# A reordered start, ropes between weight units on GpSimd, and three early down products in a hybrid decoder layer on one Trainium2 core

## The chip, the core and the metric

The kernel runs on one core of a Trainium2 chip (trn2). TensorE multiplies; VectorE (DVE in the profile), ScalarE (ACT) and GpSimd (POOL) do the rest; SyncE (SP) issues most of the DMAs. Each engine works through its own queue in order and waits on counting semaphores. The metric is the device time of one execution in microseconds (us).

## The reference

A decoder layer over 528 tokens (16 learned meta tokens and 512 of the sequence) of width 1024, in float32:

```python
h = concat([meta, x])                                   # (528, 1024)
h = h + 0.5 * swiglu(rmsnorm(h, ffn1_norm), gate, up, down)      # FFN1, D_FF = 2816
h = h + token_mixing(rmsnorm(h, mix_norm), ...)                  # mixer
h = h + 0.5 * swiglu(rmsnorm(h, ffn2_norm), gate, up, down)      # FFN2
return rmsnorm(h, final_norm)[16:]

def swiglu(h, w_gate, w_up, w_down):
    return (silu(h @ w_gate) * (h @ w_up)) @ w_down
```

`token_mixing` projects with `w_in` and runs two mixers side by side: a gated linear attention of 4 heads (`gq`, `gk`, `gv`, `gr`), and a sparse attention of 8 heads (`dq`, `dk`, `dv`), whose keys an indexer selects (the best 128 of each query's visible keys). `dq` and `dk` get rotary embeddings, `x * cos + rot(x) * sin`, with `rot` swapping the halves of each head of 64. Both results, side by side, are multiplied with `w_out`.

## The kernel before

**Splitting.** Every large product is made of three passes on values rounded to the type fp32r: the high part of the weights with the high part of the input, high with low, and low with high. ScalarE makes a high part of a weight unit (128 columns for all 1024 rows) with `hi(u)`, GpSimd the low part with `lo(u)` (line 1796), in pieces of 256 columns: four operations for a full unit, two for a down unit. `w_hi` and `w_split` count them. TensorE counts `w_used` when it is through with a unit, and this frees its place. `raw` is a ring of four slots that SP refills in the order of the units, each slot when its unit is split.

**The start.** `x` is loaded with tokens on partitions. TensorE turns it in ten steps (line 2724); VectorE copies each result out of PSUM with `keep_x(n)` (line 461) into `h`; ScalarE squares and sums; VectorE makes variance and reciprocal in two parts (`x_variance(0)` for the meta tokens and the first two tiles, `x_variance(1)` for the last two), ScalarE the root; the reciprocal roots stand on diagonals (`diag`), which TensorE multiplies with ones (`spread`, line 2712) to have them across all partitions. VectorE makes eight tiles `xn` (line 2394) from `h`, gain and spread. ScalarE makes `xh` (`high_x(d)`, line 1932) and VectorE `xl` (line 2399).

**The first four products** (`first_products`, line 2498) are gate and up of the first two plain tiles of FFN1, units 0 to 3. Each has 16 matmuls of 264 columns for each of its three passes. TensorE begins with the high passes of units 0 and 1 tile by tile, as ScalarE delivers `xh`, with unit 0's low pass two tiles behind; then the low pass of unit 1, the high passes of 2 and 3, the low passes of 2 and 3, and at last the `xl` passes of all four.

**FFNs.** The first group of four column tiles (`PLAIN = 4`) is computed plainly, the others in pairs with seven products of half size instead of eight (`SEVEN`, line 2673), with sums of weight quarters made by VectorE (`sums`, `low_pair`). The gate product is passed through Silu on ScalarE, multiplied with the up product on VectorE, and split again into `ah` (line 1946) and `al` (line 2204). The down products of the first group follow its last plain tile: four of the eight (`PRE_DOWN = 4`), each a sum over the four activation tiles. The activation of the last plain tile is the latest, so the loop over `(k0, k1, ds)` runs tiles 0 to 2 of down products 0 and 1 first, then their tile 3 (which waits for `a_lo`), and then down products 2 and 3 in full. Down product d of this group has PSUM bank 2d; banks 4 to 7 hold the last plain tile's gate and up, so that products 2 and 3 wait until that tile is out (`a_prod` in FFN1, `up_scaled` in FFN2). VectorE adds each finished down product to `h` (`add_down`, line 2229).

**The mixer.** Units in order: indexer queries (4), indexer keys, `gv` (4), `dq` and `dk` (8, `M_DQK`), `dv` (4, `M_DV`), `gq` and `gk` (4, `M_GQK`), `gr` (4), `w_out` (8). The first two DQK products and a part of the third and fourth run between the indexer's logits; then DQK 4 to 7 (48 matmuls of 264 columns each, line 2462), the four V units (30 of 512 columns, line 582), and the attention. ScalarE takes DQK product n out of PSUM into `pjb[:, n]` (`pj_kept`), SP swaps its halves by DMA into `sw[:, n % 4]` (`swap_r`: after the product's eviction, and for n of 4 and more after rope n - 4 is complete, since it reuses the buffer), and GpSimd applies the rope n in three operations: `sw * sin`, `pjb * cos`, their sum (`q_roped`). In GpSimd's queue rope n stands whole behind the low part of unit DQK 3 + n. Meanwhile VectorE selects the top keys, from 456 to 522 us, without a wait on TensorE.

**The attention.** TensorE waits for all eight ropes (`q_roped` 8), makes the first two heads' logits (line 722), and fills the rest of its time with products that the linear attention needs (`fill_step`: `M_GQK` and the first two `gr` units, one product of 8 steps for every 4 pairs of heads). The fill products have the banks of `FILL_BANK`; the first has bank 0, where V's first block was, and so waits for `v_kept` 4. The tails (`tails`, line 734), the last 16 keys' logits of the first block of queries, run after fill steps 1 and 2. `turn_probs(n, t)` turns a head's probabilities into bank 4 or 5. VectorE masks (`masked`, lines 1404 and 1409), evicts fill products (`keep_fill`), and shares the eviction of turned probabilities with ScalarE.

## Time and profile before

| | |
|---|---|
| median of 3 runs | 1056.43 us (1056.31 to 1061.72) |
| the profiled execution | 1057.6 us |
| its span, first to last instruction | 1055.8 us |
| TensorE busy | 1037.3 us, 98% |
| granted TensorE clock | 0.999 |
| GpSimd, VectorE, ScalarE busy | 659.6, 783.1, 466.8 us |
| DMA engines, mean share of the span | 32.8% |

The profiled execution is one run with the profiler on; its span leaves out 1.8 us around the instructions. PE is TensorE's matmuls, PEld its weight loads, which overlap. A matmul's end is modelled, and successive matmuls overlap, so that the distance of two starts is what one costs. In a timeline a row is a run of like instructions: start, time to the end of the last, engine, line, operation, out<-in, shapes, count, and in brackets the idle time of the engine before it and what ended that.

### The profile page before, as it was taken

The numbers are of one execution on the slowest core, as the hardware profiler recorded it, in microseconds if no ns is written. First come the engines' busy times: TensorE is split into PE (matmuls) and PEld (weight loads), VectorE is DVE, ScalarE is ACT, GpSimd is POOL, SyncE is SP. The second block draws the span as 40 slices with busy tenths as digits, with TensorE's granted clock in tenths as the row PEclk, the third lists the DMA queues.
The fourth block names the chain that finished last, engine by engine and source line by source line (L and its number), as shares of the span: only waits on it lengthen the run. The fifth ranks groups of instructions, "written<-read, shape, count | busy, mean of one in ns | idle before, by whom it ended". The sixth has DMA issues, their size and how long they took to land.

```text
span 1055.8 us, 19800 instructions
## 1 busy us (share of the span) xinstructions
PE 1037.3 (98%) x7527; PEld 947.1 (90%) x7527; DVE 783.1 (74%) x1270; ACT 466.8 (44%) x748; POOL 659.6 (62%) x747
## 2 busy tenths in 40 slices
PE   8999999999999999989999999999999999999997
PEld 8999999999999997878678788778899999999997
DVE  7557897677676587699766585478999977777835
ACT  6433444334343344562256536353544433443436
POOL 5767777787786367259732213446887877777840
PEclk9999999999999999999999999999999999999999
DMA  6243343333332444334321102222233434334322
GB/s 202 71 119 102 84 112 96 111 87 105 110 95 77 119 120 111 83 100 122 100 61 41 41 21 61 62 78 77 84 100 101 120 111 117 86 106 112 91 61 80
DMA packets 172258, 98.71 MB, mean 93 GB/s; under 512 B 6787, under 2 KB 167606, under 8 KB 172166
## 3 DMA queue, kind: packets, MB, share of 16 engines
q1 hardware_dynamic: 172064, 97.38, 32.8%
q8 instruction: 60, 0.98, 0.4%
q14 instruction: 32, 0.26, 0.1%
q10 hardware_dynamic: 102, 0.08, 0.0%
HBM read 91.18 MB, written 2.10 MB: 88 GB/s over the span
## 4 chain that ended last, share of the span: by engine, by line
PE 89%; POOL 4%; DVE 2%; ACT 2%; issue 2%; DMA 0%; SPq 0%; DVEq 0%; ACTq 0%; POOLq 0%
PE ps L2462 37%; PE ps L2673 34%; PE ps L582 5%; PE ps L596 4%; POOL wl L1796 2%; PE ps L766 1%; PE ps L722 1%; PE ps L2498 1%; PE ps L745 1%; PE ps L878 1%; POOL pjb L1879 1%; POOL sw L1876 1%; POOL pjb L1877 1%; PE ps L2724 1%; DVE xn L2394 1%
## 5 line engine op out<-in xcount | busy, mean ns | idle before, releaser
L1796 POOL TENSOR_TENSOR wl<-raw,wh 128x256 fp32r<-128x256 f32 x292 | 249.4, 888 | 203.2 <-ACT wh L1905 167.3
L1796 POOL TENSOR_TENSOR wxl<-raw,wxh 128x256 fp32r<-128x256 f32 x240 | 231.2, 988 | 136.6 <-ACT wxh L1905 136.1
L2462 PE MATMUL ps<-ah,wxh 128*128 128x264 f32 (+2 forms) x464 | 123.2, 319 | 0.4 <-DVE al L2204 0.4
L2462 PE MATMUL ps<-ah,wxl 128*128 128x264 f32 (+2 forms) x464 | 123.0, 318 | 0.0
L2462 PE MATMUL ps<-al,wxh 128*128 128x264 f32 (+2 forms) x464 | 122.9, 318 | 0.0
L2673 PE MATMUL ps<-xh,wh 128*128 128x264 f32 (+1 forms) x360 | 101.9, 283 | 0.0
L2673 PE MATMUL ps<-xl,wh 128*128 128x264 f32 (+1 forms) x360 | 101.9, 283 | 0.0
L2673 PE MATMUL ps<-xh,wl 128*128 128x264 f32 (+1 forms) x360 | 101.5, 282 | 0.0
L2229 DVE SCALAR_TENSOR_TENSOR h<-ps,h 128x528 f32<-128x528 f32 (+1 forms) x88 | 61.0, 694 | 51.9 <-PE ps L2462 51.8
L2462 PE MATMUL ps<-xh,wh 128*128 128x264 f32 (+3 forms) x304 | 94.5, 349 | 4.7 <-POOL wl L1796 3.5
L2462 PE MATMUL ps<-xl,wh 128*128 128x264 f32 (+3 forms) x304 | 90.8, 337 | 0.0
L2462 PE MATMUL ps<-xh,wl 128*128 128x264 f32 (+3 forms) x304 | 90.7, 337 | 0.0
L1905 ACT ACTIVATE wxh<-raw 128x512 fp32r<-128x512 f32 (+2 forms) x88 | 53.4, 607 | 73.5 <-PE ps L2462 72.8
L2462 PEld LDWEIGHTS ps<-ah,wxl 128*128 128x128 f32 x464 | 77.1, 188 | 6.3
L2462 PEld LDWEIGHTS ps<-ah,wxh 128*128 128x128 f32 x464 | 77.1, 188 | 5.7 <-DVE al L2204 0.9
L2462 PEld LDWEIGHTS ps<-al,wxh 128*128 128x128 f32 x464 | 77.2, 188 | 4.8
L1796 POOL TENSOR_TENSOR wl<-ws,wh 128x256 fp32r<-128x256 f32 x72 | 69.9, 1001 | 9.5 <-ACT wh L1923 9.5
L1946 ACT ACTIVATE ah<-ubuf 128x528 fp32r<-128x528 f32 (+1 forms) x36 | 23.0, 640 | 110.7 <-DVE ubuf L2337 100.1
L1905 ACT ACTIVATE wh<-raw 128x1024 fp32r<-128x1024 f32 (+1 forms) x61 | 57.9, 968 | 23.5 <-PE ps L582 18.1
L2673 PEld LDWEIGHTS ps<-xh,wh 128*128 128x128 f32 x360 | 67.8, 188 | 0.4
L2673 PEld LDWEIGHTS ps<-xl,wh 128*128 128x128 f32 x360 | 67.8, 188 | 0.4
L2673 PEld LDWEIGHTS ps<-xh,wl 128*128 128x128 f32 x360 | 67.9, 189 | 0.0
(322 smaller groups left out, 3016.7 us busy)
## 6 DMA issues: line engine op xcount, KB each, us to landing
raw<-in_ffn_w_gate SPq DMA_DIRECT2D x44, 512.0 KB, 4.1
raw<-in_ffn_w_up SPq DMA_DIRECT2D x44, 512.0 KB, 4.9
raw<-in_ffn_w_down SPq DMA_DIRECT2D x80, 256.0 KB, 2.8
raw<-in_w_in SPq DMA_DIRECT2D x28, 512.0 KB, 4.2
raw<-in_w_out SPq DMA_DIRECT2D x8, 512.0 KB, 3.4
xin<-in_x SPq DMA_DIRECT2D x4, 512.0 KB, 5.7
raw<-in_ffn_w_down SPq DMA_DIRECT2D x16, 128.0 KB, 2.2
out<-xin SPq DMA_DIRECT2D x4, 512.0 KB, 3.5
```

Of the source, the lines that this page charges most:

```text
L582: mm = pe.matmul(ps[0:n, V_BANKS[m0][b], :], xx[:, 2 * q + k, s:s + n], ww[:, slot, k * 512:(k + 1) * 512], start=(q == 0 and k == 0 and c ...
L596: return pe.matmul(ps[:, bank, :], ww[:, slot, k * 256 + dd * P:k * 256 + (dd + 1) * P], rr[:, tile, META:TOK], start=(starts and k == 0 a ...
L722: pe.matmul(ps[0:w, qk_bank(n), 0:main_keys(b)], pjb[e:e + HD, pair, s:s + w], pjb[e:e + HD, 4 + pair, 0:main_keys(b)], start=True, stop=T ...
L745: mm = pe.transpose(ps[0:wc, 4 + t % 2, c * w:(c + 1) * w], lg[0:w, n % 4, sc:sc + wc], ident[0:w, 0:w])
L766: mm = pe.matmul(o[HD * e:HD * (e + 1), :], dv[0:wc, c, (hd + e) * HD:(hd + e + 1) * HD], pt[0:wc, (n + e) % 3, c * w:(c + 1) * w], start= ...
L878: mm = pe.matmul(ps[:, lv_bank(g) + e, c:c + 64], x, x.rearrange("p (m a b) -> p m a b", a=2, b=LEVELS[g - 1])[:, :, 1, :], start=True, st ...
L1796: op = pool.tensor_tensor(dst[:, part], src[:, part], high[:, part].bitcast(F32), ALU.subtract)
L1905: act.activation(places(0, PLACE[u], c)[:, 0:n], raw[:, slot, 0:n], ACT.Copy).then_inc(w_hi, c)
L1946: act.activation(ah[:, j, tk], src, ACT.Copy).then_inc(a_hi, 1)
L2229: dve.scalar_tensor_tensor(out=as_parts(h[:, d, tk], norm), in0=psum_parts(bank, norm), scalar=0.5, in1=as_parts(h[:, d, tk], norm), op0=A ...
L2462: mm = pe.matmul(ps[0:m, bank + a, 0:width], places(lo, PLACE[u], -(-WIDTH[u] // HALF_UNIT))[:, k * P:k * P + m], r[:, tile, t:t + width], ...
L2673: mm = pe.matmul(ps[:, seven_bank(v, i), 0:w], places(lo, at_p[wn], 1)[:, k * P:(k + 1) * P], x_operand(xlo, xn_, w, number)[:, k, :], sta ...
```

## The change

It has three parts.

1. The start. VectorE's `keep_x(8)` goes to ScalarE, behind the last two diagonals and ahead of `hi(0)`; `x_variance(1)` comes after `keep_x(6)` instead of after `keep_x(7)`; `high_x(0)` stands between `hi(0)` and `hi(1)`. In TensorE's loop unit 1's high pass is one tile behind unit 0's. The `xl` passes of units 0 and 1 come ahead of the low pass of unit 2, and that of unit 2 ahead of the low pass of unit 3.
2. The mixer. GpSimd's low part of DQK 4 comes ahead of rope 0; after it, two of the ropes' 24 operations stand between two low parts, three from V 1 on, and the last two behind the low part of `M_GQK` + 1. The first fill product has bank 5 and no wait for `v_kept` 4 (the second, in bank 1, has it now); the second head's turned probabilities, in bank 5, wait for its eviction; the tails run after fill steps 2 and 3.
3. Both FFNs. Tiles 0 to 2 of three down products instead of two run ahead of tile 3.

```diff
@@ keep_x
+            if n == X_BY_ACT:                                   # X_BY_ACT = 8
+                eng.activation(dst, src, ACT.Copy).then_inc(x_kept_act, 1)
+            else:
+                eng.tensor_copy(dst, src).then_inc(x_kept, 1)
@@ ScalarE, start
+            keep_x(act, X_BY_ACT)
             hi(0)
+            high_x(0)
             hi(1)
-            for d in range(KT):
+            for d in range(1, KT):
                 high_x(d)
@@ VectorE, start
             for n in range(10):
-                keep_x(dve, n)
+                if n != X_BY_ACT:
+                    keep_x(dve, n)
...
-                if n == 7:
+                if n == 6:
                     x_variance(1)
...
-            dve.wait_ge(x_kept, 10)
+            dve.wait_ge(x_kept, 9)
+            dve.wait_ge(x_kept_act, 1)
@@ first_products
                 for k in range(KT + 2):
                     if k < KT:
                         part(0, k, 0)
-                        part(1, k, 0)
+                    if k >= 1 and k <= KT:
+                        part(1, k - 1, 0)
                     if k >= 2:
                         part(0, k - 2, 1)
-                for v, lo in ((1, 1), (2, 0), (3, 0), (2, 1), (3, 1)):
+                for v, lo in ((1, 1), (2, 0), (3, 0)):
                     for k in range(KT):
                         part(v, k, lo)
-                for v in range(4):
+                low_inputs(0)
+                low_inputs(1)
+                for v in (2, 3):
                     for k in range(KT):
-                        mm = part(v, k, 0, True)
-                    mm.then_inc(w_used, 2)
+                        part(v, k, 1)
+                    low_inputs(v)
@@ GpSimd, mixer
-            for n in range(8):
-                lo(U_MIX + M_DQK + 3 + n)
-                pool.wait_ge(swapped[5 + n], 64)
...
-            lo(U_MIX + M_DV + 3)
-            lo(U_MIX + M_GQK)
+            def rope_steps(first, last):                        # operation i is step i % 3 of rope i // 3
...
+            lo(U_MIX + M_DQK + 3)
+            lo(U_MIX + M_DQK + 4)
+            for n in range(4):
+                rope_steps(2 * n, 2 * n + 2)
+                lo(U_MIX + M_DQK + 5 + n)
+            rope_steps(8, 10)
+            for n in range(4):
+                lo(U_MIX + M_DQK + 9 + n)
+                rope_steps(10 + 3 * n, 13 + 3 * n)
             lo(U_MIX + M_GQK + 1)
+            rope_steps(22, 24)
             lo(U_MIX + M_GQK + 2)
@@ attention
-            FILL_BANK = [0, 1, 0, 0, 0, 1]
+            FILL_BANK = [5, 1, 0, 0, 0, 1]
...
-                    if m == 0:
+                    if m == 1:
                         pe.wait_ge(v_kept, 4)
...
                 if t >= 2:
                     turn_free(pe, t - 2)
+                elif t == 1:
+                    pe.wait_ge(gqk_scaled, 1)
...
-                if k in (1, 2):
-                    tails(k - 1)
+                if k in (2, 3):
+                    tails(k - 2)
@@ FFN, down products of the first group
-                for k0, k1, ds in ((0, PLAIN - 1, range(2)), (PLAIN - 1, PLAIN, range(2)), (0, PLAIN, range(2, PRE_DOWN))):
+                for k0, k1, ds in ((0, PLAIN - 1, range(3)), (PLAIN - 1, PLAIN, range(3)), (0, PLAIN, range(3, PRE_DOWN))):
```

In all parts the same values are computed; only their order and the engine of one copy differ.

## Rows read from the trace of the kernel before

**Rows 1.** the page, busy time of each engine (share of the span, instructions)
```profile
PE 1037.3 (98%) x7527; PEld 947.1 (90%) x7527; DVE 783.1 (74%) x1270; ACT 466.8 (44%) x748; POOL 659.6 (62%) x747
```

**Rows 2.** TensorE's waits: line waited for; us in total, times, longest
```profile
PE ps L2462 <- POOL wl L1796: 3.5, 3, 2.3
PE ps L2498 <- POOL wl L1796: 2.0, 1, 2.0
...
PE ps L2462 <- ACT pjb L1055: 0.7, 1, 0.7
PE ps L582 <- POOL wl L1796: 0.6, 1, 0.6
```

**Rows 3.** TensorE in three stretches: us, busy (matmuls), granted clock, DMA
```profile
31.53:41.33 9.80, 9.80 (x80) 1.00 0.19 55
...
495.71:523.54 27.83, 27.83 (x120) 1.00 0.42 110
475.57:481.39 5.82, 5.82 (x47) 1.00 0.51 138
```

**Rows 4.** GpSimd's timeline from 20 us: start, duration, what, [idle before it]
```profile
20.97 10.51 POOL L1796 TENSOR_TENSOR wl<-raw,wh 128x256 fp32r<-128x256 f32 x8 [0.48 <-ACT wh L1905]
```

**Rows 5.** VectorE's timeline of the start
```profile
19.18 8.31 DVE L2399 TENSOR_TENSOR xl<-xn,xh 128x528 fp32r<-128x528 f32 x8
...
9.97 1.89 DVE L461 COPY h<-ps 128x512 f32<-128x512 f32 x3
...
13.77 1.44 DVE L2394 SCALAR_TENSOR_TENSOR xn<-h,vecs,ps 128x528 f32<-128x528 f32 x2 [0.35 <-PE ps L2712]
```

**Rows 6.** ScalarE's timeline of the start, to 15.9 us
```profile
12.41 0.69 ACT L2084 ACTIVATE diag<-ident,xvar 128x128 f32<-128x128 f32 x2
13.01 1.99 ACT L1905 ACTIVATE wh<-raw 128x1024 fp32r<-128x1024 f32 x2
14.90 1.16 ACT L1932 ACTIVATE xh<-xn 128x528 fp32r<-128x528 f32 x2
```

**Rows 7.** ScalarE's timeline around the mixer's first DQK copies
```profile
457.47 0.62 ACT L1051 ACTIVATE pjb<-ps 128x512 f32<-128x512 f32 x1
457.95 1.09 ACT L1905 ACTIVATE wh<-raw 128x1024 fp32r<-128x1024 f32 x1
```

**Rows 8.** TensorE's timeline of the start
```profile
6.26 3.67 PE L2724 MATMUL ps<-ident,xin 128*128 128x128 f32 x16
...
9.72 2.00 PE L2724 MATMUL ps<-ident,xin 128*128 128x128 f32 x16
...
15.67 1.74 PE L2498 MATMUL ps<-xh,wh 128*128 128x264 f32 x12 [1.14 <-ACT xh L1932]
```

**Rows 9.** GpSimd's timeline of the ropes and low parts
```profile
462.06 1.30 POOL L1876 TENSOR_TENSOR sw<-sw,cs 128x512 f32<-128x512 f32 x1 [11.30 <-DMA sw<-pjb]
...
465.96 2.79 POOL L1796 TENSOR_TENSOR wl<-raw,wh 128x256 fp32r<-128x256 f32 x4
...
488.85 1.34 POOL L1876 TENSOR_TENSOR sw<-sw,cs 128x528 f32<-128x528 f32 x1
...
513.18 8.43 POOL L1796 TENSOR_TENSOR wl<-raw,wh 128x256 fp32r<-128x256 f32 x12
```

**Rows 10.** TensorE's timeline, the first matmul of the first fill product
```profile
525.06 0.47 PE L2462 MATMUL ps<-xh,wh 128*128 128x512 f32 x1 [0.41 <-ACT dv L1063]
```

**Rows 11.** VectorE's timeline, the first operation after the top-k work
```profile
529.38 0.18 DVE L1404 CUSTOM_DVE_ANT_0 lg<-ps,mask 100x16 f32<-100x16 f32 x1 [7.18 <-PE ps L734]
```

**Rows 12.** TensorE's timeline, FFN2's last plain tile
```profile
747.33 0.50 PE L2462 MATMUL ps<-ah,wxh 128*128 128x512 f32 x1 [0.43 <-DVE al L2204]
```

**Rows 13.** VectorE's timeline at FFN2's and at FFN1's last plain tile
```profile
743.51 0.68 DVE L2266 TENSOR_TENSOR t<-ps,rstd 128x512 f32<-128x512 f32 x1
...
70.11 0.71 DVE L2229 SCALAR_TENSOR_TENSOR h<-ps,h 128x528 f32<-128x528 f32 x1 [0.35 <-PE ps L2462]
```

**Rows 14.** GpSimd's timeline behind FFN2's last plain tile
```profile
750.39 4.70 POOL L1796 TENSOR_TENSOR wl<-ws,wh 128x256 fp32r<-128x256 f32 x4 [3.66 <-ACT wh L1923]
```

More of the change, by code:

```diff
@@ L454, in build @@
         X_BANKS, VEC_BANK = 6, 4
+        X_BY_ACT = 8
         def keep_x(eng, n):
@@ L1442, in keep_fill @@
                 else:
-                    bank = [0, 1, 0, 0, 0, 1, 6, 7][m]
+                    bank = [5, 1, 0, 0, 0, 1, 6, 7][m]
                     dst = pja[:, 4 + m, :] if m < 4 else gr[(m - 4) // 2][:, m % 2, :]
@@ L1869, in _ @@
                 lo(U_MIX + M_DQK + n)
-            for n in range(8):
-                lo(U_MIX + M_DQK + 3 + n)
-                pool.wait_ge(swapped[5 + n], 64)
-                c = META if n < 4 else 0
-                s, r = sw[:, n % 4, c:], pjb[:, n, c:]
-                pool.tensor_tensor(s, s, sinr[:, c:], ALU.mult).then_inc(q_part, 1)
-                pool.tensor_tensor(r, r, cosr[:, c:], ALU.mult).then_inc(q_part, 1)
-                pool.wait_ge(q_part, 2 * (n + 1))
-                pool.tensor_tensor(r, r, s, ALU.add).then_inc(q_roped, 1)
-            lo(U_MIX + M_DV + 3)
-            lo(U_MIX + M_GQK)
+            def rope_steps(first, last):
+                for i in range(first, last):
+                    n, step = divmod(i, 3)
+                    c = META if n < 4 else 0
+                    s, r = sw[:, n % 4, c:], pjb[:, n, c:]
+                    if step == 0:
+                        pool.wait_ge(swapped[5 + n], 64)
+                        pool.tensor_tensor(s, s, sinr[:, c:], ALU.mult).then_inc(q_part, 1)
+                    elif step == 1:
+                        pool.tensor_tensor(r, r, cosr[:, c:], ALU.mult).then_inc(q_part, 1)
+                    else:
+                        pool.wait_ge(q_part, 2 * (n + 1))
+                        pool.tensor_tensor(r, r, s, ALU.add).then_inc(q_roped, 1)
+            lo(U_MIX + M_DQK + 3)
[7 more added lines that the diff above has]
+                rope_steps(10 + 3 * n, 13 + 3 * n)
             lo(U_MIX + M_GQK + 1)
+            rope_steps(22, 24)
             lo(U_MIX + M_GQK + 2)
@@ L2501, in part, with low_inputs @@
                     return mm
+                def low_inputs(v):
+                    for k in range(KT):
+                        mm = part(v, k, 0, True)
+                    mm.then_inc(w_used, 2)
                 for k in range(KT + 2):
```

3 lines of the change are left out of this document (1 added, 2 removed).

## The prediction

> **What bounds the kernel now.** I read first the page's busy shares. TensorE's matmuls fill 98% of the span [rows 1], so the time is the sum of TensorE's work and of its stalls, and an edit pays only where it removes a stall of TensorE or adds one. Nothing in the diff removes a matmul. The second view was therefore the waits of TensorE alone. They are few and short, and most of them lie where the diff is [rows 2]: one of 2.0 us among the first four products, on GpSimd's low part of a weight unit; three (3.5 us together), one of 0.6 us and one of 0.7 us around the DQK and V units of the mixer; and two of 0.4 us, on `dv` and on `al`, of which below. These 7.6 us are what can be won.
>
> An idle time in these rows runs from the modelled end of the last matmul, not from the moment at which the next could have started. A 264-column matmul lasts 0.28 us in the rows and starts every 0.1225 us (9.80 us for 80), a 512-column one starts every 0.232 us (27.83 us for 120) [rows 3]. So each gap loses some 0.16 us more than its idle time, and the first matmul after it is slow by some hundredths: I add 0.2 us per gap.
>
> Third came the timelines of the engines that end those waits.
>
> **The start.** GpSimd makes the low parts of units 2 and 3 in eight operations of 1.31 us, to 31.48 [rows 4]; TensorE gets the last at 31.53 [rows 3] and could have had it 2.2 us earlier. After the change the products of `xl` with units 0 and 1 (32 matmuls, 3.9 us at the rate of [rows 3]) stand ahead of unit 2's low part and 16 more ahead of unit 3's. With the 48 matmuls of the interleaved loop done at 21.9 (below) and 1.96 us for each 16, unit 2's low part is wanted at 31.7 and unit 3's at 35.7, 4 us after it is there. The `xl` tiles are now wanted from 27.8 on instead of from 33.6; VectorE has made the last of the eight by 27.49 [rows 5]. The stall goes: 2.0 + 0.2 = 2.2 us.
>
> Against that stands ScalarE's new order. VectorE's copies out of PSUM take 1.89/3 = 0.63 us each, and the variance comes one copy earlier, so the root and the two diagonals of ScalarE end at 12.5 instead of 13.1 [rows 6]. Then ScalarE has `keep_x(8)`: the trace has no such copy there; the nearest one is 0.62 us long [rows 7], and neighbours overlap by 0.09 us. I take 0.53; ends 0.5 and 1.0 (that of a conversion twice as large). So `hi(0)` starts at 12.95, as before (13.01). It takes 0.95, and `high_x(0)` follows at once at 14.0 (VectorE's first `xn` needs 0.76 and starts at some 13.2, when both the spread and the ScalarE copy are there): TensorE starts at 14.75, 0.9 us earlier than at 15.67 [rows 8]. But it gets two matmuls only. `hi(1)` stands between `high_x(0)` and `high_x(1)`, and the second tile is there at 16.1 instead of 16.06, TensorE goes on at 16.24. From there 46 of the 48 matmuls of the interleaved loop remain, 5.65 us, to 21.9; before, 48 from 15.67 came to 21.6. The later `xh` tiles come every 0.54 (1.16 less 0.62) to 0.68 us (VectorE's pace, 1.44 less 0.76) and a step of three products takes 0.73, so they hold nothing up. The early start is worth nothing and the interleaving costs 0.3 us. Net gain at the start 1.9 us (1.2 to 2.3).
>
> Does it last? Behind the first products the weight conversions, ScalarE's Silu and the loads all hang on counts that TensorE or GpSimd gives, and in FFN1 TensorE has no listed wait. The shift is handed on.
>
> **GpSimd's ropes.** Before, GpSimd has made the low part of DQK 3 by 450.8 and then sits 11.3 us until the swapped rows of rope 0 land at 462.06 [rows 9]. The high part of DQK 4 is there at 459.04 [rows 7], but its low part is queued behind rope 0, runs at 465.96 to 468.75, and TensorE stalls 2.3 us for it. Then each turn of one rope (3.9 us) and one low part (2.8 us) is 6.7 us against TensorE's 5.9 us for a product of 48 matmuls (5.82 us for 47 [rows 3]), so it stalls 0.6 us four times more. That the row of 0.7 us names `pjb` hides this: it stands in the same beat of 6.7 us.
>
> After: low part of DQK 4 at 459.1 to 461.9, in the idle time. Then two thirds of a rope (2.6 us) between low parts: 5.4 us a turn, under 5.9. Low parts of DQK 5, 6, 7 are done at 467.5, 472.8, 478.2 and wanted at 472.4, 478.3, 484.1 (TensorE can start DQK 4 at 468.9 less the stall, 466.5, and takes 5.9 each); that of V 0 is done at 483.6 and wanted at 490.0; V 1 to 3 with three operations between (6.8 us a turn) at 489, 496, 503, wanted at 497, 504, 511. All five stalls go: 4.7 + 5 x 0.2 = 5.7 us.
>
> What is late next is the last rope, since three low parts more now stand ahead of its end. From 462.06 GpSimd has four ropes of 3.9 us, four of 528 columns at 4.0 (3 x 1.34) and nine low parts of 2.8 (8.43 us for three): 15.6 + 16.0 + 25.2 = 56.8 us, to 518.9. TensorE is through V at 523.54 - 5.7 = 517.8 and waits for `q_roped` 8 before the first logits: a new wait of some 1.1 us. Gain at the first logits 4.6 us (3.6 to 5.7). The swaps on SP are not in the way: swap n waits for its product's eviction and for rope n - 4, and the last is issued at about 492 for a rope that begins at about 511. Loads now queue behind earlier low parts, thus earlier.
>
> `FILL_BANK[0] = 5` lets the first fill product start without `v_kept` 4: the 0.41 us before 525.06 [rows 10] go. The tails, one step later, wait for `v_kept` 6 at 520.4 (four copies of 0.6 us after V) and start at 522.3: nothing. VectorE's first masked logits come at about 525.1 instead of 529.38; its top-k work was done 7.2 us before those [rows 11], at 522.2, so it isn't the bound, with 2.9 us to spare. The new wait of the second head's transposes for `gqk_scaled` 1 is on an eviction that VectorE makes right after the fill product, 1.8 us ahead. Sum of this part 5.0 us (3.8 to 6.1).
>
> **Three down products.** In FFN2 TensorE runs two products of three tiles, then waits 0.43 us for the low part of the last activation (747.33 [rows 12]). A third one (9 matmuls, 2.1 us) covers this. It needs the last up product scaled, 743.51 + 0.68 = 744.2 [rows 13], and is reached at 746.7. Gain 0.6 us. Behind it GpSimd's low part for the second of the seven products lands at 755.09 [rows 14] and would be wanted at 755.15: up to 0.1 us comes back. In FFN1 there is no stall to cover: the first finished down product comes 2.2 us later, VectorE's add of 70.11 [rows 13] waits for it, and its `low_pair` slides to 75.5, still ahead of 79.4 where TensorE wants it. Worth 0. This part: 0.6 us (0 to 0.7).
>
> **Sum.** 1.9 + 5.0 + 0.6 = 7.5 us off the profiled execution's 1057.6, which gives 1050.1. That execution lies 1.2 us above the median of the runs, 1056.43: forecast 1049.0 us. At the good ends the gain is 9.4 us (1047.0), at the bad ends 5.0 (1051.4).
>
> **Rivals.**
> (a) A new wait of TensorE takes back 2 to 5 us: GpSimd ends its ropes later than 518.9, or a low part is late in the attention. For it: the margin there is already negative by 1.1 us. Against: all its prices are start to start in the same stretch. 1051 to 1054, some 1052.5.
> (b) VectorE sets the pace of the attention, so that what TensorE wins ahead of it is lost there. For it: the masks and half of the transposed probabilities are its work. Against: its idle time of 7.2 us [rows 11], and that TensorE has one wait of over 0.15 us on it in the first half of the attention. Only 1.9 + 0.6 stay: 1053.9.
> (c) The clock. TensorE runs the same transposes every 0.22 us (3.67 for 16) up to 9.7 and every 0.115 us (2.00 for 16) from there on [rows 8], the low and the full level of 1.2 and 2.4 GHz. After the change TensorE does little between 13.9 and 16.2: its two new matmuls stand alone in a gap of 2.3 us, where it was idle for 1.14 us before. If the clock fell there for as long as it was low at first (8.3 us from its first matmul), half of that is lost: 4.2 us, 1053.2. The Trainium skill, "TensorE: Matmul & The Clock Gate", section "HAM oscillation — how this bites in real kernels", says that idle stretches between bursts can put the array back to the lower clock. The trace shows none after the stall of 2.3 us at 466.6: the granted clock is 1.00 in the stretches behind it [rows 3]. That speaks against (c).
> (d) Slower than before: GpSimd is slowed in the ropes' stretch as it is at 20.97, where an operation takes 1.31 instead of 0.70 us beside VectorE [rows 4]. Its 56.8 us would have to grow by 7.5 us, 13%, to eat the whole gain; if the 36 operations of the nine low parts took 1.31, it is 22 us, and the time 1071. Against: the order alone is new, and the top-k work ran beside GpSimd's 0.70 us through the whole stretch. The Trainium skill, "SBUF — State Buffer", section "Who interferes with whom", says that a VectorE operation with two SBUF inputs and a GpSimd operation that reads SBUF block one another. The trace agrees at the start, where 1.31 us stand beside `xl` with its two inputs. The ropes' end at 518.9 lies inside the top-k work, before its end at 522.2.
>
> **From these to the numbers.** Forecast with its own ends 0.70 (range 1047.0 to 1051.1), (a) 0.12, (b) 0.09, (c) 0.04, (d) 0.05. A measurement tells 0.5% (5.3 us) from no change, so the border is at 1051.1. Faster: 0.70 and less than half of (a), 0.75. Same: the rest of (a), (b) and (c), 0.20. Slower: 0.05. The range takes in (a): 1046.8 to 1053.0; (b), (d) and part of (c), under 0.2, stay out.
>
> **What would show it.** Start: no idle time of TensorE on `wl` at 29 to 32; two matmuls at 14.7 and the next at 16.2; the first matmul of the third gate product at 39.4 instead of 41.3. Mixer: no wait on GpSimd between the DQK units; one new wait of about 1 us in front of the first logits, on GpSimd's `pjb`; fill product begins without a gap. FFN2: no wait on `al`. Wrong would be: an idle time in front of the logits of over 3 us, a new wait on the low parts of V units, a lower granted clock between 14 and 20 us, or new waits of TensorE on VectorE in the attention.

## The result, and the profile after

The changed kernel took 1050.12 us in the median of 6 runs (1049.34 to 1057.75), the one before 1057.02 (1056.26 to 1061.72); the ratio is 0.9944, with an interval of 0.9926 to 0.9961. The forecast was 1049.0 us, with a range of 1046.8 to 1053.0. Built once more for the experiments, the same kernel had a ratio of 0.9963 (0.9949 to 0.9977), and its executions lay between 1049.31 and 1056.76. So the gain is real, it is 4 to 6 us, and single executions differ by more than that. Where this spread comes from turned out to be the larger part of the study. A ratio here is not the quotient of the two medians beside it (1050.12 / 1057.02 would be 0.9935), so nothing should be read from a difference of 0.001 between the two. Two executions, one of `ropes_alone` with 1119 us at a mean granted clock of 0.85 and one of `after_s1_early` with 1259 us at 0.75, are left out of the ratios.

The profiled execution took 1050.75 us, with a span of 1049.0, against 1057.6 and 1055.8 before. First the page's busy times and then TensorE's waits, which answer to [rows 1, 2]:

```profile
PE 1036.0 (99%) x7527; PEld 946.5 (90%) x7527; DVE 779.9 (74%) x1269; ACT 467.0 (45%) x749; POOL 657.4 (63%) x747
```

```profile
PE ps L2525 <- ACT xh L1955: 1.8, 2, 0.9
...
PE ps L727 <- POOL pjb L1892: 1.0, 1, 1.0
...
PE ps L2489 <- POOL wxl L1804: 0.3, 1, 0.3
```

All waits on the low parts `wl`, 6.1 us in five places before, are gone, and with them the 0.7 us put down to `pjb` in the same beat. New are a second wait on `xh` at the start, one of 1.0 us on the last rope, and one of 0.3 us on a down unit's low part, `wxl`.

The same stretches of TensorE's work before and after give the balance. Each boundary is the start of the same matmul in both traces. The windows of after, for TensorE alone (from:to, length, busy with the number of matmuls, granted clock, DMA share, GB/s):

```profile
15.29:39.90 24.61, 24.61 (x191) 0.93 0.34 98
...
39.90:465.04 425.14, 424.74 (x3218) 1.00 0.36 100
465.04:517.24 52.20, 51.17 (x314) 1.00 0.50 134
...
517.24:526.05 8.81, 8.81 (x44) 1.00 0.25 70
...
526.05:735.81 209.76, 207.79 (x1512) 1.00 0.18 55
735.81:746.91 11.10, 11.10 (x49) 1.00 0.10 28
746.91:760.40 13.49, 13.18 (x97) 1.00 0.42 117
760.40:1041.69 281.29, 281.29 (x2023) 1.00 0.34 96
```

| stretch | before, us | after, us | gain |
|---|---|---|---|
| start to the end of the first four products | 41.33 | 39.90 | 1.43 |
| to DQK 4 | 425.14 | 425.14 | 0 |
| DQK 4 to 7 and V, to the first logits | 57.07 | 52.20 | 4.87 |
| first logits and first fill product | 9.28 | 8.81 | 0.47 |
| attention, FFN2's plain tiles | 209.76 | 209.76 | 0 |
| FFN2's early down products and the tile behind | 11.82 | 11.10 | 0.72 |
| the next seven products of FFN2 | 12.76 | 13.49 | -0.73 |
| FFN2's rest | 281.29 | 281.29 | 0 |

The sum is 6.76 us. Three long stretches, 916 us, came out the same to 0.01 us: TensorE hands a shift on unchanged, and whatever differs does so in the few places that the diff touches. The last part's gain is given back in the very next stretch. And in the first row of the windows the granted clock is 0.93.

**The start.** TensorE's timeline (start, duration, line, operation, count, idle time before and what ended it), and a window for it alone, from the fall of the clock to its rise:

```profile
13.90 0.48 PE L2525 MATMUL ps<-xh,wh 128*128 128x264 f32 x2 [0.85 <-ACT xh L1955]
15.29 1.02 PE L2525 MATMUL ps<-xh,wh 128*128 128x264 f32 x3 [0.91 <-ACT xh L1955]
```

```profile
15.33:18.75 3.42, 3.42 (x16) 0.50 0.48 132
```

Two matmuls stand alone between two idle times, as forecast. Then TensorE's clock is at its low level of 1.2 GHz for 3.4 us, right behind the second idle time; from 18.75 on it is 2.4 GHz again. The stretch from the third matmul to the end takes 24.61 us. An execution without this fall (`after_repeat`, below) takes 23.13: the fall costs 1.5 us.

**The mixer.** GpSimd's low part of DQK 4, and at the end that of the second GQK unit and the last two rope steps; then TensorE's first logits:

```profile
457.69 2.84 POOL L1804 TENSOR_TENSOR wl<-raw,wh 128x256 fp32r<-128x256 f32 x4 [8.35 <-ACT wh L1928]
...
511.67 2.83 POOL L1804 TENSOR_TENSOR wl<-raw,wh 128x256 fp32r<-128x256 f32 x4
514.47 1.34 POOL L1889 TENSOR_TENSOR pjb<-pjb,cs 128x528 f32<-128x528 f32 x1
515.88 1.30 POOL L1892 TENSOR_TENSOR pjb<-pjb,sw 128x528 f32<-128x528 f32 x1
```

```profile
517.24 1.11 PE L727 MATMUL ps<-pjb 64*100 64x512 f32 x4 [1.03 <-POOL pjb L1892]
```

The low part of DQK 4 now fills GpSimd's idle time, and the last rope ends at 517.2. TensorE, done with V, waits 1.03 us for it. VectorE's first masked logits, for [rows 11]:

```profile
523.32 0.17 DVE L1412 CUSTOM_DVE_ANT_0 lg<-ps,mask 100x16 f32<-100x16 f32 x1 [3.98 <-PE ps L739]
```

VectorE is still early, but with 4.0 us to spare where it had 7.2.

**FFN2.** TensorE and GpSimd behind the last plain tile, for [rows 12, 14]:

```profile
751.80 0.51 PE L2489 MATMUL ps<-ah,wxh 128*128 128x512 f32 x1 [0.31 <-POOL wxl L1804]
```

```profile
743.64 4.69 POOL L1804 TENSOR_TENSOR wl<-ws,wh 128x256 fp32r<-128x256 f32 x4 [3.66 <-ACT wh L1946]
748.29 8.63 POOL L1804 TENSOR_TENSOR wxl<-raw,wxh 128x256 fp32r<-128x256 f32 x6
```

The wait on `al` is gone. 4.9 us after the early products, TensorE waits for the low part of the fifth down unit: its two pieces are the first two of the six `wxl` operations and end at 751.75. Before the change they ended at 758.50 and TensorE wanted them at 758.66.

### The profile page after: what moved, and what is told of

It is laid out like the page before. It is cut to its first block, busy times and chain, and to the rows that moved or that the text cites. A ratio compares the mean times of both kernels' runs of the same rounds, so it can differ in the third digit from the quotient of the medians.

```text
span 1049.0 us, 19801 instructions
## 1 busy us (share of the span) xinstructions
PE 1036.0 (99%) x7527; PEld 946.5 (90%) x7527; DVE 779.9 (74%) x1269; ACT 467.0 (45%) x749; POOL 657.4 (63%) x747
## 4 chain that ended last, share of the span: by engine, by line
PE 86%; POOL 6%; ACT 2%; DVE 2%; issue 2%; DMA 1%; SPq 0%; DVEq 0%; ACTq 0%; POOLq 0%
PE ps L2489 36%; PE ps L2709 34%; PE ps L601 4%; POOL wl L1804 3%; PE ps L587 3%; PE ps L2525 2%; PE ps L774 1%; PE ps L727 1%; POOL pjb L1892 1%; POOL sw L1887 1%; POOL pjb L1889 1%; PE ps L753 1%; PE ps L886 1%; DMA xin<-in_x 1%; PE ps L927 0%
## 5 line engine op out<-in xcount | busy, mean ns | idle before, releaser
L1804 POOL TENSOR_TENSOR wl<-ws,wh 128x256 fp32r<-128x256 f32 x72 | 67.3, 967 | 9.5 <-ACT wh L1946 9.5
```

The lines of the kernel that those rows point to most:

```text
L1804: op = pool.tensor_tensor(dst[:, part], src[:, part], high[:, part].bitcast(F32), ALU.subtract)
```

## Experiments

Twelve kernels were run in four groups; each group had its own runs of the kernel before on the same chip, and the ratios are against those.

### The three parts, each alone

`mixer_alone` is the kernel before with part 2 of the change, `start_alone` with part 1, `down_alone` with part 3. The last one's edit:

```diff
-for k0, k1, ds in ((0, PLAIN - 1, range(2)), (PLAIN - 1, PLAIN, range(2)), (0, PLAIN, range(2, PRE_DOWN))):
+for k0, k1, ds in ((0, PLAIN - 1, range(3)), (PLAIN - 1, PLAIN, range(3)), (0, PLAIN, range(3, PRE_DOWN))):
```

> The kernel before with the second part of the change alone (GpSimd's ropes between low parts, bank 5 for the first fill product, tails a step later). My theory, from the profile after the change: this part carries 5.3 us of the whole, so 1057.0 becomes 1051.7 (ratio 0.995). The trace should show the new wait of 1.0 us on the last rope before the first logits. Rival, that VectorE's pace in the attention or something behind it takes part of it back: under 4 us.

> The kernel before with the first part alone (start). My theory: removing the stall on unit 3's low part gives 2.2 us, the interleaving takes 0.3 us, and where the granted clock falls to the lower level behind the two lone matmuls another 1.5 us are lost in that execution. So 1.9 us faster in executions with a clock of 0.999 and 0.4 us in those with 0.997. Rival: the fall of the clock is chance and has nothing to do with the new idle times; then it is seen as often in runs of the kernel before.

> The kernel before with the third part alone (three down products ahead of the last activation's tile). My theory, from the profile after the change: the stall of 0.43 us on the activation's low part goes, and TensorE waits the same time longer for the low part of the fifth down unit, so 0.0 us. As predicted before the result was known: 0.6 us faster. In the trace the idle time on wxl behind the third of the seven products tells them apart, 0.3 us or none.

| kernel | median, us | before, us | ratio | interval |
|---|---|---|---|---|
| `mixer_alone` | 1052.35 | 1056.45 | 0.9958 | 0.9939 to 0.9977 |
| `start_alone` | 1057.8 | 1056.45 | 0.9999 | 0.9988 to 1.0011 |
| `down_alone` | 1057.57 | 1056.45 | 1.0000 | 0.9991 to 1.0009 |

The mixer's part carries the gain: 4.4 us (0.0042 of 1056), under the 5.3 of the theory and over the rival's bound of 4. Its profile has the new wait, 1.3 us on `pjb`.

The down products are worth nothing. (The medians lie 1.1 us apart because the executions of both kernels fall into two groups, at 1056.1 to 1056.6 and at 1057.5 to 1058.1, and the median stands in one or the other; of this below.) Their wait is moved, as TensorE's waits and timeline in `down_alone` show: no row on `al` any more, and

```profile
757.50 0.50 PE L2462 MATMUL ps<-ah,wxh 128*128 128x512 f32 x1 [0.31 <-POOL wxl L1796]
```

The start's part has a ratio of 0.9999 too, although in its profile the first four products end at 39.64 instead of 41.33. That profile has a fall of the clock, but elsewhere, directly behind the stall of 2.25 us on DQK 4's low part, which this kernel still has at 467 us:

```profile
466.96:470.37 3.41, 3.17 (x14) 0.50 0.64 181
```

Of its 12 executions two took 1054.5 us at a mean granted clock of 0.998, three 1055.8 to 1056.1 at 0.997, and seven 1057.8 to 1058.4 at 0.996 to 0.997. One fall of 3.4 us lowers the mean by 0.0016, so the means fit one fall more in the seven than in the two. They don't prove it: in every profile the clock is also at its low level for the last 1.1 to 4.2 us, when TensorE has no matmul left; this costs nothing, but lowers the mean by 0.0005 to 0.0020. Of the 3.3 us between the fastest executions and the seven, some 1.1 can be a late first rise of the clock (last section) and 1.5 a fall at the start; the rest is open, and none of the seven has a trace. So the question became what brings the falls, and `start_old_interleave` was made for it.

### The interleaving at the start

`after_old_interleave` is the changed kernel with units 0 and 1 in step again:

```diff
             hi(0)
-            high_x(0)
             hi(1)
-            for d in range(1, KT):
+            for d in range(KT):
                 high_x(d)
...
                     if k < KT:
                         part(0, k, 0)
-                    if k >= 1 and k <= KT:
-                        part(1, k - 1, 0)
+                        part(1, k, 0)
```

> The changed kernel with two details of its start undone: high_x(0) stands behind hi(1) again, and unit 1's high pass runs beside unit 0's again. All else, the copy on ScalarE and the new order of the xl passes too, stays. My theory: TensorE starts once, without a gap in the middle, the 0.3 us come back, and the granted clock does not fall at 15 to 19 us; 1050.1 becomes 1049.1 in the median, and 0.3 us against executions of the changed kernel with a clock of 0.999. Rival: the early start is worth its place, and this is 0.5 us slower.

The kernel took 1049.41 us in the median, ratio 0.9925 (0.9910 to 0.9941), the best of all kernels, though its interval overlaps that of the changed kernel's first runs (0.9926 to 0.9961) and leaves only that of `after_repeat` (from 0.9949) apart; four of its six executions lay between 1049.37 and 1049.43. TensorE's idle time is one of 1.6 us instead of two, no fall follows it, and the first four products end at 38.15. The profile is of the one execution of 1053.55 us; its 4.2 us above the others are about a wait of 2.77 us for VectorE (last section) and a fall of the clock right behind that wait, at 528.11. `start_old_interleave` puts the same two edits on `start_alone`:

> The start's part alone on the kernel before, without its interleaving: the copy of the ninth turned tile on ScalarE and the new order of the four products behind the first loop, but units 0 and 1 in step and ScalarE's second weight unit ahead of the first activation tile, as before. The start's part with its interleaving had a ratio of 0.9999, though in its profile the first four products end 1.9 us earlier; the mean granted clock of most of its executions was 0.996 where the kernel before has 0.998 to 0.999. My theory: the stall of 2.2 us for the low part is gone in both, and the interleaving's gaps are what lowers the clock in most executions (1.5 to 1.7 us for each fall of 3.4 us). Then this kernel runs at 0.998 to 0.999, and is 1.9 to 2.3 us shorter than the one before: 1054.2 to 1055.7 us, ratio 0.998. Rival: an earlier arrival at the stall of 2.25 us at 467 us, or another place in the mixer, meets the falls, whatever the first loop is; then the ratio is again 0.999 to 1.000 and the clock 0.996 to 0.997.

It took 1054.9 us (1054.11 to 1055.38) beside 1057.66 for the kernel before, ratio 0.9975 (0.9965 to 0.9984), where `start_alone` had 0.9999. The intervals don't touch. TensorE's timeline and the window of the first four products:

```profile
14.69 1.49 PE L2506 MATMUL ps<-xh,wh 128*128 128x264 f32 x10 [1.61 <-ACT xh L1937]
```

```profile
14.69:38.07 23.38, 23.38 (x192) 1.00 0.39 110
```

Without the interleaving the start's part is worth 2.6 us (0.0025 of 1057), and the interleaving takes that away again. That the fastest executions of the two kernels lie only 0.4 us apart (1054.11 and 1054.49) says how: the interleaving costs 0.4 us where nothing else happens, and the rest lies in how often the executions of some microseconds more come. My theory's direction held; that falls of the clock are what makes these longer is argued from the profiles with a fall, as said. One of its numbers didn't hold: the mean clock is 0.997 to 0.998, not 0.998 to 0.999, and this profile too has one fall, at 452.8 us. Behind it the kernel waits for GpSimd's low parts anyway: the stall of 2.3 us is 0.7 here. A fall ahead of a stall is hidden in it.

`after_warm` fills both idle times with matmuls that nothing reads (nine `keep_warm` instead of four behind the spread, eight between the first two product matmuls and the third):

```diff
+                    if k == 1:
+                        keep_warm(8)
...
-            keep_warm(4)
+            keep_warm(9)
```

> The changed kernel with nine instead of four filler matmuls behind the spread and eight more between the first two product matmuls and the third, so that TensorE is not idle between 13.9 and 15.3 us; the fillers write a bank that nothing reads. If the fall of the granted clock at 15.3 us in the changed kernel's profile comes from the idle time in front of it, the first four products end at the full rate, 38.2 to 38.6 us where the changed kernel's profile has 39.9, and the kernel is up to 1.5 us shorter than the changed one in those executions in which the fall is there. Rival: the fall comes with or without the gap (as it did at 453 and at 528 us elsewhere); then the fillers cost 0 to 0.4 us and the median is that of the changed kernel.

Its timeline:

```profile
13.91 0.49 PE L2525 MATMUL ps<-xh,wh 128*128 128x264 f32 x2
14.24 1.95 PE L2737 MATMUL ps<-ident,ones 128*128 128x128 f32 x16
15.94 0.73 PE L2525 MATMUL ps<-xh,wh 128*128 128x264 f32 x4
```

There is no fall at the start, and the products end at 39.02, against 39.90. But the fillers run to 15.94 where the second tile is there at 15.29, so 0.65 of the 1.5 us are spent on them. The five executions agree to 0.4 us (1049.94 to 1050.33; ratio 0.9935, 0.9922 to 0.9947), and the median is that of the changed kernel. `warm_rope_first` has fillers cut to the gaps (eight behind the spread, four between the products), and the ropes' end first, of which next:

> The changed kernel with the new interleaving, the last rope steps first, and fillers cut to the gaps at the start (eight behind the spread, four between the first two product matmuls and the third; 112 ns for each of their two passes), so that they end at 15.1 us, ahead of the second tile at 15.3. If the fillers keep the clock and cost nothing, the first four products end 0.2 to 0.6 us earlier than with the longer fillers (39.0 in that profile) and the kernel takes 1048.3 to 1048.7 us. Rival: any work of TensorE in the gap delays the tile by its own queue and the interleaving still costs 0.3 us against the old one: 1048.7 to 1049.2.

Ratio 0.9938 (0.9925 to 0.9951), median 1049.82, above both what was expected and its rival, and with 1048.22 the shortest execution of all kernels. Its profile has no fall before the last microseconds. The first four products take 23.17 us from the third matmul, at 16.56, to 39.73; `after_repeat`, whose clock rose as late, has 16.53 and 39.66. So short fillers cost nothing that shows. The spread from 1048.2 to 1051.8 at the same mean clock is more than the 1.1 us of a late rise, and stays unexplained.

`after_repeat` is the changed kernel once more.

> The changed kernel once more, on the chip of the other two, to compare with. If the fall of the granted clock behind the gap at the start is a property of the new interleaving, this profile shows it again within 1 us of the third product matmul and the first four products take 24.6 us from there as they did (23.1 us without it). Rival: the fall was an accident of one execution; then none is seen before 20 us and the products end at 38.4 to 38.6 us when the clock rises early.

Median 1052.26, ratio 0.9963 (0.9949 to 0.9977). Here the rival was right for the profile: the two gaps are there, and no fall behind them.

```profile
16.53:39.66 23.13, 23.13 (x191) 1.00 0.36 103
```

So in these traces the gaps make the fall possible and not certain. Of the five profiles with the two gaps three have it (`after` at 15.33, `after_rope_first` at 17.95, `after_s1_early` at 16.69, each within 0.8 us of the third matmul), two don't; of the two with fillers and the seven with one gap none has it. What else decides is open.

`after_repeat` has a fall at 453.41. Five other profiles have one between 452.8 and 457.0 (`after_warm`, `old_rope_first`, `after_old_interleave`, `start_old_interleave`, `after_s1_early`), the other eight have none there. TensorE's timeline:

```profile
451.58 2.14 PE L688 MATMUL ps<-ikga,wa 16*128 16x264 f32 x8 [0.32 <-ACT gb L1098]
453.65 0.79 PE L2489 MATMUL ps<-xh,wh 128*128 128x512 f32 x1
454.25 0.63 PE L2489 MATMUL ps<-xl,wh 128*128 128x512 f32 x1
```

An idle time of 0.3 us and eight matmuls over 16 rows stand there, in every profile; behind them the 512-column matmuls take 0.42 us from start to start, instead of the 0.23 of the rows behind 457. Here too the same code is followed by a fall in one execution and not in another.

### The wait before the logits

`ropes_alone` is the kernel before with GpSimd's order only, without the fill product's bank and the later tails.

> The kernel before with only GpSimd's order of ropes and low parts changed. The mixer's part alone gave a ratio of 0.9958; of its 4.9 us at the logits all should be the order's and 0.4 to 0.5 us behind them the fill product's bank. So this one gains 4.5 to 4.9 us at the first logits, keeps the idle time of 0.4 us ahead of the fill product (TensorE on VectorE's last V copy), and its median is 0.4 us above that of the mixer's part alone. Rival: the bank and the later tails are needed for the gain, because without them TensorE waits for VectorE's V copies longer than before: then the wait ahead of the fill product grows to over 1 us and the gain is below 4 us.

Ratio 0.9961 (0.9948 to 0.9974), where `mixer_alone` had 0.9958. Its timeline at the logits:

```profile
517.55 1.10 PE L722 MATMUL ps<-pjb 64*100 64x512 f32 x4 [1.04 <-POOL pjb L1884]
518.59 0.50 PE L2477 MATMUL ps<-xh,wh 128*128 128x512 f32 x1
```

The new wait is the same, and the fill product follows 1.04 us after the logits' start without an idle time, bank 0 or not. In `mixer_alone` these are 519.12 and 520.16, again 1.04. Both the expectation and its rival were wrong: the 0.41 us of [rows 10] went because TensorE stood 1 us for the rope, in which VectorE's copies of V were done. The bank and the tails are worth nothing in this order.

`after_rope_first` has the last two rope steps ahead of the second GQK unit's low part:

```diff
-            lo(U_MIX + M_GQK + 1)
             rope_steps(22, 24)
+            lo(U_MIX + M_GQK + 1)
```

> The changed kernel with GpSimd's last two rope steps ahead of the low part of the second GQK unit. My theory of the new wait: the 1.0 us that TensorE waits for the last rope before the first logits is there only because three low parts more stand ahead of that rope's end. Then the rope ends some 2.8 us earlier (at about 514.4 where it was 517.2), TensorE finds it done, and the kernel is 1.0 to 1.2 us shorter than the changed one: 1048.2 to 1049.1 us, ratio to the kernel before about 0.992 to 0.993, with no wait on GpSimd in front of the logits. Rival, VectorE sets the pace there: VectorE's first masked logits wait for its own top-k work, so the wait only changes its name (TensorE on VectorE at the second pair's transposes) and the time stays at that of the changed kernel, 1049.3 to 1050.1.

The wait is gone, and nothing takes its place. GpSimd, TensorE, and the window from the matmul behind `gb` to the first product with `dv` (busy times of PE, PEld, DVE, ACT, POOL, then TensorE's clock):

```profile
515.06 1.33 POOL L1892 TENSOR_TENSOR pjb<-pjb,sw 128x528 f32<-128x528 f32 x1
516.35 2.82 POOL L1804 TENSOR_TENSOR wl<-raw,wh 128x256 fp32r<-128x256 f32 x4
```

```profile
518.19 1.10 PE L727 MATMUL ps<-pjb 64*100 64x512 f32 x4
```

```profile
453.88:531.88 78.00, 77.74 (x436) 62.70 (x437) 73.24 (x226) 32.82 (x46) 64.45 (x72) 1.00 0.45 122
```

The changed kernel takes 79.09 us for the same stretch (451.83 to 530.92): 1.09 us saved, as forecast, and the rival of VectorE falls. Yet the median is 1049.95, ratio 0.9936 (0.9923 to 0.9949), outside the 1048.2 to 1049.1 expected and not better than the changed kernel by anything that can be told. The profiled execution, of 1051.75 us, has the fall at 17.95, which has nothing to do with the ropes. `old_rope_first`, which adds the old interleaving, shows what else there is.

> The changed kernel with the old interleaving of the first two products and GpSimd's last two rope steps ahead of the low part of the second GQK unit. My theory: the stall before the logits is worth 1.1 us and the old interleaving keeps the clock up behind the start, so most executions take 1048.2 to 1048.5 us, 1.1 below the changed kernel's best, and the profile shows no fall of the granted clock before 20 us and no wait on GpSimd's rope. Rival: the two executions of 1049.8 and 1051.8 us seen with the ropes first mean that this order costs elsewhere what it wins at the logits (the second GQK unit's low part 2.8 us later): then the time stays at 1049.4 or above.

Median 1050.23, ratio 0.9937 (0.9924 to 0.9950), no gain, so the rival's number is what came. Its reason is another one, though: the second GQK unit's late low part makes no wait. This profile has a fall at 454.59, and takes 79.56 us for the stretch, 1.56 more than `after_rope_first` without a fall. `after_repeat`, with the ropes' old end and a fall at 453.41, takes 79.52 for it (451.58 to 531.10) and shows no wait before its logits. With a fall at 453 us TensorE comes late to the rope and the wait vanishes in it; taking the wait away then wins nothing. It is worth 1.1 us only where the clock stays up. How many of the executions without a trace have that fall isn't known.

### The down products

`after_s1_early` lets VectorE make the first of the four weight sums ahead of the last activation's low part, where it was idle 0.77 us:

```diff
                         dve.tensor_tensor(t1[:, tk], t0[:, tk], t1[:, tk], ALU.mult).then_inc(a_prod, 1)
+                        if j == PLAIN - 1:
+                            sums(U_PAIR[number, 1, 0], 1)
                         dve.wait_ge(a_prod, o + 1)
...
-                sums(U_PAIR[number, 1, 0])
+                sums(U_PAIR[number, 1, 0], 2 if number else 3)
```

> The changed kernel with the first of the four weight sums of the fifth down unit (FFN2) made by VectorE in its idle 0.8 us ahead of the last activation's low part. My theory of the down products: three products ahead win 0.7 us and the fifth unit's low part, made by GpSimd 11.2 us after the last activation's, takes it back as a wait of 0.3 us and a slowed piece of 0.4. With one VectorE operation less in that chain the low part comes 0.6 to 1.1 us earlier, the wait of 0.3 us is gone and the piece behind the pre-products is 12.8 instead of 13.5 us: the kernel is some 0.6 us shorter than the changed one. Rival: GpSimd is held by other work (its operations of 1.7 us beside VectorE's two-input ones), not by the chain behind the activation: then the wait stays and the time is the changed kernel's.

The rival was nearer. The wait on `wxl` stays at 0.3 us, and from the matmul behind the wait on `pjb` (643.53 in the changed kernel) to the end of this wait it is 108.11 us against 108.27: 0.16 instead of 0.6. VectorE's timeline says why:

```profile
741.43 1.23 DVE L2200 TENSOR_TENSOR ws<-raw 128x512 f32<-128x512 f32 x1
742.58 1.22 DVE L2232 TENSOR_TENSOR al<-t,ah 128x512 fp32r<-128x512 f32 x1
743.72 0.68 DVE L2203 TENSOR_TENSOR ws<-raw 128x512 f32<-128x512 f32 x1
```

The moved sum takes 1.23 us and not the 0.68 of its neighbour, at a time when GpSimd works on low parts (738.54 to 743.25); it ends behind the idle time and delays `al`. Its ratio was 0.9958 (0.9946 to 0.9970); that it lies above the changed kernel's first 0.9944 can't be told from `after_repeat`'s 0.9963.

## Why the prediction was right, and where not

**The sum** was 7.5 us off the profiled execution, and 6.85 came. Two accidents of that execution stand in it, an early rise of the clock that wins some 1.1 us (below) and the fall that costs 1.5; without both it is some 7.2. The forecast of 1049.0 lies 0.3 us under the changed kernel's best executions, 1.1 under its first median, and 3.3 under that of `after_repeat`, 1052.26, which is past the sum's own ends (1047.0 to 1051.1) and inside the range only because this takes in rival (a), whose cause no trace shows. So part of the closeness is luck. "Faster" was given 0.75 against a border of 0.5%: the first ratio is past it with 0.56%, the second is not with 0.37%, so this can't be called decided. One addition is off as well: the good ends of the three parts, 2.3, 6.1 and 0.7, add up to 9.1 us and not 9.4.

**The start.** The stall of 2.2 us is gone, and the two matmuls stand alone as forecast. With the clock up and as late a rise as before, the products end at 39.66 against 41.33: 1.7 us (1.9 forecast). What is missing is in ScalarE's first `xh` in `after_repeat`:

```profile
14.35 0.64 ACT L1955 ACTIVATE xh<-xn 128x528 fp32r<-128x528 f32 x1 [0.49 <-DVE xn L2421]
```

It was forecast at 14.0 and waited for VectorE's tile, so the third matmul started at 16.53 and not at 16.24. Without the interleaving the gain is 2.1: 38.15 and 38.07 against 40.24 and 40.18 in `ropes_alone` and `down_alone`, all four with an early rise. So the interleaving costs the 0.3 to 0.4 us of the sum while the clock stays up. What the sum lacked is the clock: rival (c) had the place and the size of the gap right and the chance wrong. I gave it 0.04 and a fall of 8.3 us for 4.2. It comes in three of five profiles, for 3.4 us, and costs 1.5. The step that failed was the reason against it, that the trace showed no fall behind the stall at 466.6 (there was none, though the stretches of [rows 3] begin 9 us behind it). `start_alone` fell behind this very stall. One execution in which the clock held is no evidence that it holds. A lower granted clock between 14 and 20 us was named as a sign of being wrong, and it came. The Trainium skill, "TensorE: Matmul & The Clock Gate", section "HAM oscillation — how this bites in real kernels", warns of idle stretches between bursts (its example has longer ones than the 0.85 and 0.91 us here); the traces agree where the granted clock is 0.50 at 15.33 to 18.75, and disagree where the same two gaps were followed by 1.00.

**The ropes.** 4.6 us were forecast at the first logits and 4.87 came; the new wait was put at 1.1 us and is 1.03 (1.27 in `mixer_alone`). The prices were distances of starts in the same stretch, beside the same work of the other engines, and they carried over: a queue of 60 GpSimd operations, put at 56.8 us, took 56.6 (460.63 to 517.18). VectorE's top-k work, forecast to end at 522.2, was done at 519.34, which is why 4.0 us were to spare and not 2.9.

**The fill product.** 0.4 forecast, 0.47 measured, right by luck, for the reason was wrong: `ropes_alone` shows that the rope's wait hides VectorE's copies and the bank does nothing. I counted a wait as removed by an edit, when the wait put in front of it had covered it already.

**The down products.** 0.6 forecast, 0 measured, in the trace and in `down_alone`. This is the step of the sum that failed. I followed the early products to the next low part, that for the second of the seven products (755.09 against 755.15), and left it at up to 0.1 us. The next one in GpSimd's queue, the fifth down unit's, had 0.16 us to spare (758.50 against 758.66). A stage that is won by 0.7 us is only won if everything queued behind it on the engines that feed it comes earlier too; here the whole chain, from the last activation through VectorE's sums and ScalarE's high parts to GpSimd, hangs on a time that the edit doesn't move.

**Rivals (a), (b), (d).** GpSimd wasn't slowed in the ropes, and the new wait on the rope was not longer than forecast; the one of 0.3 us on `wxl`, in FFN2, was not forecast. (b), VectorE as the bound in the attention, isn't so in the changed kernel's profiles, but it was in one execution of `after_old_interleave`, as the last section shows.

## What to carry to other kernels

After a stall is removed, follow the chain that fed it, and every later transfer or split in the same queue, until one is found that has more slack than the stall was worth. Price an edit in the order that all the others leave behind, since a new wait can cover an old one. And where TensorE gets a lone matmul or two between two idle times, count a fall of the clock as a cost that comes in some executions: begin the burst later and whole. Filling the gap with work kept the clock up here too, but won nothing in the median.

## What the runs showed of the hardware

**The clock rises and falls at other places in each execution.** It rose at 5.1 to 6.0 us in six of the fourteen profiles and at 9.6 to 11.1 in eight, and the first product starts some 1.1 us earlier after an early rise (14.61 against 15.67 with the same code). TensorE's transposes show it: in `down_alone` they start every 0.11 us from 6.08 on, where the kernel before has 0.22 up to 9.7 [rows 8].

```profile
6.08 2.87 PE L2724 MATMUL ps<-ident,xin 128*128 128x128 f32 x24
```

The runs of the kernel before lie in two groups, but for a few, at 1056.1 to 1056.6 and at 1057.5 to 1058.1. The profile of 1057.6 us has a late rise (9.9) and that of `down_alone`, of 1056.54, an early one (5.8); that all executions divide this way is inferred from these two.

**VectorE and GpSimd can shut each other out for longer than one operation.** In `after_old_interleave`'s profile two VectorE operations on the mask in the middle of the top-k work, with one SBUF input each, last 9.20 us. The changed kernel's profile has 1.14 for them. First VectorE, then GpSimd in the same stretch:

```profile
477.96 9.20 DVE L1391 TENSOR_SCALAR mask<-mask 100x228 f32<-100x228 f32 x2
487.09 0.59 DVE L1381 MAX8 small<-mask 100x8 f32<-100x428 f32 x1
```

```profile
482.70 2.84 POOL L1804 TENSOR_TENSOR wl<-raw,wh 128x256 fp32r<-128x256 f32 x4
485.48 1.31 POOL L1889 TENSOR_TENSOR pjb<-pjb,cs 128x512 f32<-128x512 f32 x1
486.86 1.45 POOL L1892 TENSOR_TENSOR pjb<-pjb,sw 128x512 f32<-128x512 f32 x1
```

The first of the two lasts 8.96 us and ends, at 486.92, just behind a pause of 0.08 us that GpSimd makes after a row of operations without a break (486.79 to 486.86; it waits there for its own product). In the other thirteen profiles this operation lasts 0.27 to 0.88 us and ends 0.17 to 0.28 us behind the start of a GpSimd operation, the first since its own start. Here it missed ten of those changes; the top-k work ended at 525.7 instead of 519.3, 6.4 us later and so by more than the 4 us to spare, and TensorE waited:

```profile
527.62 0.74 PE L727 MATMUL ps<-pjb 64*100 64x512 f32 x2 [2.77 <-DVE small L1417]
```

That is rival (b), in one execution. The new order of the ropes gives it more room: the operation that waits for its own engine's product came every 6.7 us before, and between 472.63 and 488.78 the changed GpSimd has no such pause, 16 us. It fits the seven executions of 1055 to 1058 us that `mixer_alone`, `ropes_alone` and the changed kernel have; but no kernel was run that puts a pause back, so this cause of theirs is argued, not shown; falls of the clock are the rival (five of the seven have a mean of 0.994 to 0.997, two 0.998 and 0.999).

The other way round, `after_s1_early` has a GpSimd operation of 5.56 us at 19.11, usually 0.7, beside VectorE operations with two inputs back to back:

```profile
19.11 5.56 POOL L1804 TENSOR_TENSOR wl<-raw,wh 128x256 fp32r<-128x256 f32 x1
```

```profile
19.05 5.03 DVE L2431 TENSOR_TENSOR xl<-xn,xh 128x528 fp32r<-128x528 f32 x8
24.12 1.66 DVE L2250 TENSOR_TENSOR xn<-xn 128x1056 f32<-128x1056 f32 x1
```

VectorE's first pause, of 0.03 us, is at 24.1; the operation ends at 24.67, and TensorE waits 0.7 us for it. Mostly the two take turns: in the changed kernel both slow to 1.2 us an operation there. The Trainium skill, "SBUF — State Buffer", section "Who interferes with whom", says of the port pair that the two share that whoever issues first has it for the whole instruction and the other is blocked; the traces agree for most operations (1.2 us each, where the start-to-start time of one engine's alone is 0.62 and 0.70), and show these two blocked across a row of the other's instructions, up to the first pause.
